# Latent attention, restructured: heads projected in blocks of four, scores unsplit, modulation products on VectorE

## The chip, the cores and the metric

One core of a Trainium2 chip runs the whole network of two layers. The metric is the time of one execution in device microseconds. Before the change it is 1305.78 us, the median of three runs (1305.38 to 1312.1).

## The reference

A diffusion backbone of two layers over 256 context tokens and 256 latent tokens, width 1024, all in fp32. Layer 0 mixes tokens with multi-head latent attention, layer 1 with a Mamba-2 scan; behind each comes a SwiGLU FFN, and a norm ends it. The change touches layer 0's attention and its modulation:

```python
proj = h @ w_in                                   # 512 tokens, 1024 -> 512 + 256 + 32
cq, ckv, kr = split(proj)
q  = (rms_norm(cq, q_norm) @ w_uq)                # 16 heads of 64 + 32 (rotary)
kv = (rms_norm(ckv, kv_norm) @ w_ukv)             # 16 heads: k_nope 64, v 64
# rotary positions on q_rope and kr of the latent tokens only
k = concat(k_nope, broadcast(kr)); q = concat(q_nope, q_rope)
out_x = softmax(q_latent @ k.T / sqrt(96)) @ v @ w_o          # keys: all 512 tokens
out_c = softmax(q_ctx @ k_ctx.T / sqrt(96)) @ v_ctx @ w_o     # keys: 256 context tokens
```

The modulation (shift, scale and gate of each sub-layer) is `silu(c) @ ada_w[i] + ada_b[i]`, 6144 columns for each of two conditioning vectors.

## The kernel before

Everything is kept transposed: features on partitions, 512 tokens on the free axis. A matmul in full precision is made of three fp32r passes (`three`, lines 1498 to 1502): each operand is split into a high and a low part, and low x high, high x high and high x low are summed in a bank. Weights stream through a ring of four buffers: the SP queue loads block n into `raw` (`load`, line 288), ScalarE copies it to `w_hi` (`hi`, line 565), VectorE subtracts to `w_lo` (`lo`, line 963), TensorE uses it and frees it. Each engine's program is an order written out by hand, and engines meet at semaphores.

Attention begins with seven tiles of the input projection (24 matmuls each), two for ckv, one for the rotary key, four for cq. ckv is normed among them. Then the v tiles of all heads are made, while cq's norm runs (a reciprocal of 128x512, a multiplication by the row and a split for each of four tiles), and then the heads follow one after the other. In step i (`head`, lines 771, 1132 and 1714) TensorE projects head i+1 (12 matmuls for q with the swapped rotary features beside it, 6 for k, with 64 columns of weights), transposes the probabilities of head i (12 transposes), does 16 small products for the modulation (`ada_two`, heads 0 to 11), computes the scores of head i+1 in split form (two tiles of 512 keys for the latent queries, two of 256 for the context) and multiplies head i's probabilities with v (`values`, 24 matmuls). ScalarE copies q and k out of the banks, makes their high parts, copies the transposed probabilities, and takes the exponentials of head i+1 with their sums. VectorE rotates q, makes k's low part, splits weights, takes the maxima, inverts the sums and makes the low half of the output. POOL makes q's low part (`q_low`, line 450), scales the probabilities (`scale_probs`, line 437) and copies one head of v.

After the heads follow eight tiles of the output projection, the second norm and the FFN. During the FFN VectorE computes 56 vectors of modulation by `matvec` (line 1039): two products of 128x1024 with a row of silu(c), each with its sum; one such pair gives 128 modulation values for both conditionings. The modulation of layer 0 that attention's output and the FFN's input need is made on TensorE (16 tiles ahead of attention, 24 in the heads).

Of the kernel before, what the change touches and what calls it, by code (L numbers as in the profile page):

```python
# [33 lines left out]
QKD = 96  # L34
# [22 lines left out]
TAB = {"ident": 0, "gt": 128, "lt": 256, "le": 384, "ge": 512, "cos": 640, "sin": 896}  # L57
NTAB = 1152
# [5 lines left out]
HL = HP + 2  # L64
WO = HL + 2 * 15
# [11 lines left out]
ADA1 = 40  # L77
VEC = 56
# [10 lines left out]
def block_cols():  # L89

    cols = [1024] * NBLK
    for i in range(-1, 15):
        n = HP if i < 0 else HL + 2 * i
        cols[n], cols[n + 1] = 512, 128
    cols[DT] = 512
    return cols
# [4 lines left out]

NORM_K = [8, 2, 4, 8, 8, 16, 8, 8]
SPLIT = {3: (5, 6, 7), 4: (7,)}
NB = [sum(k for v, k in enumerate(NORM_K[:w]) if v not in SPLIT) for w in range(len(NORM_K) + 1)]
# [29 lines left out]
def program(nc, a, out):  # L134
# [9 lines left out]
    with ExitStack() as fixed:  # L144
# [20 lines left out]
        gain = [sb(f"gain{i}", [128, 8, 2]) for i in range(4)]  # L165
        bank = [fixed.enter_context(nc.psum_tensor(f"bank{i}", [128, 512], f32)) for i in range(8)]
# [8 lines left out]
        with ExitStack() as ph:  # L175
            Hmh, Hml = (sb(f"mla_h_{p}", [128, KD, TOK], f32r, ph) for p in ("hi", "lo"))
            Oh, Ol = Hmh, Hml
            cq = sb("cq", [128, KQ + KKV, TOK], f32, ph)
            kf = sb("k_rope", [128, TOK], f32, ph)
            cnh, cnl = (sb(f"c_normed_{p}", [128, KQ + KKV, TOK], f32r, ph) for p in ("hi", "lo"))  # L180
            qf = sb("q_f32", [128, TOK], f32, ph)
            qh, ql = (sb(f"q_{p}", [128, TOK], f32r, ph) for p in ("hi", "lo"))
            kh, kl = (sb(f"k_{p}", [128, TOK], f32r, ph) for p in ("hi", "lo"))
            v = sb("v", [128, 4, 64 * HEADS], f32, ph)
            vs = sb("v_head", [128, 2, 4, 64], f32, ph)

            P, rtmp = T[:, 5:8, :], T[:, 4, 0:LAT]
            ada_mla = [cq[:, 2 + 2 * r:4 + 2 * r, :].rearrange("p a n -> p (a n)") for r in range(2)]
# [7 lines left out]
        with ExitStack() as ph:  # L196
            H0h, H0l = (sb(f"ffn0_h_{p}", [128, KD, TOK], f32r, ph) for p in ("hi", "lo"))
            U0h, U0l = (sb(f"ffn0_hidden_{p}", [128, KH, TOK], f32r, ph) for p in ("hi", "lo"))
            vec_w = [T[:, 4 + 2 * r:6 + 2 * r, :].rearrange("p a n -> p (a n)") for r in range(2)]
            crow = sb("silu_c_rows", [128, 2, 1024], f32, ph)  # L200
            vec_prod = sb("matvec_products", [128, 1024], f32, ph)
# [48 lines left out]
        ada_in = [sem(f"ada_in{i}") for i in range(2)]  # L250
# [9 lines left out]
        kr_part, kr_done, kr_hi, kr_lo = sem("kr_part"), sem("kr_done"), sem("kr_hi"), sem("kr_lo")  # L260
        q_cp, rope_part, q_rope, q_hi, q_lo = sem("q_copied"), sem("rope_part"), sem("q_roped"), sem("q_hi_"), sem("q_lo_")
        k_hi, k_lo, v_out, v_mm, v_cp = sem("k_hi_"), sem("k_lo_"), sem("v_out"), sem("v_mm"), sem("v_cp")
# [24 lines left out]
        def _(sp):  # L287
# [9 lines left out]
            def ada(t, r, dst):  # L297

                sp.wait_ge(ada_used, t - 1)
                sp.dma_start(dst[r % 2], one("ada_w", t)).then_inc(ada_in[r % 2], 16)  # L300
# [18 lines left out]
            for t in range(2, 7):  # L319
                load(IN + t, IN + t, 1024, one("w_in", t))  # L320
            for t in range(2):
                load(VB + t, VB + t, 1024, one("w_uv", t))
            load(HP, HP, 512, one("w_uq", 0))
            load(HP + 1, HP + 1, 128, one("w_uk", 0))
            def queries(i, u):
                n, s = HL + 2 * (i - 1), HL + 2 * u
                load(n, s, 512, one("w_uq", i))
                load(n + 1, s + 1, 128, one("w_uk", i))

            def ada_head(i):  # L330
                for r in range(2):
                    ada(ADA0 + 2 * i + r, r, ada_mla)

            queries(1, 0)
            sp.dma_start(crow[:, :, :], a["crow"]).then_inc(crow_in, 16)
            sp.wait_ge(nlo, NB[3])
            with sp.Fori(0, 6) as j:
                for u in range(2):
                    queries(2 * j + u + 2, 1 - u)
                    ada_head(2 * j + u)  # L340
            for u in range(2):
                queries(14 + u, 1 - u)
            for t in range(8):
# [6 lines left out]
            def two(j):  # L350
                for r in range(2):
                    if late(j, 1):
                        sp.wait_ge(vec_used, 2 * j + r - 1)
                    sp.dma_start(vec_w[r], one("vec_w", 2 * j + r)).then_inc(vec_in[r], 16)
# [45 lines left out]
        def _(pool):  # L400
            nc.gpsimd.memset(scm[:, :, :], 0.0).then_inc(ones_set, 1)
            nc.gpsimd.memset(ones[:, :], 1.0).then_inc(ones_set, 1)
            nc.gpsimd.memset(eps[:, :], EPS).then_inc(ones_set, 1)

# [32 lines left out]
            def scale_probs(i, u):  # L437

                pool.wait_ge(rcp, 3 * i + 1)
                if late(i, 2):  # L440
                    pool.wait_ge(o_mm, i - 1)
                nc.gpsimd.tensor_tensor(P[:, 0, :], P[:, 0, :], rs_[:, 0:1].to_broadcast([128, 512]), MUL).then_inc(p_norm, 1)
                nc.gpsimd.tensor_copy(vs[:, u, :, :], v[:, :, ds(64 * i, 64)]).then_inc(v_cp, 1)
# [6 lines left out]
            def q_low(i):  # L450

                pool.wait_ge(q_hi, i + 1)
                nc.gpsimd.tensor_tensor(ql[0:QKD, :], qf[0:QKD, :], qh[0:QKD, :].bitcast(f32), SUB).then_inc(q_lo, 1)  # L453

            pool.wait_ge(v_out, 8)
            q_low(0)
            for i in range(2):
                scale_probs(i, i)
                q_low(i + 1)
            with pool.Fori(1, HEADS // 2 - 1) as i:  # L460
                for u in range(2):
                    scale_probs(2 * i + u, u)
                    q_low(2 * i + u + 1)
            scale_probs(14, 0)
            q_low(15)
            scale_probs(15, 1)
# [94 lines left out]
        def _(act):  # L561
# [136 lines left out]

            whole = [(0, 0, TOK)]
            for t in range(7):  # L700
                act.wait_ge(w_used, IN + t + 1)
                if t == 2:
                    A(kf[64:96, :], bank[0][64:96, :], ACT.Copy).then_inc(proj_out, 1)
                else:
                    c = t if t < 2 else t - 1
                    square(1 if t < 2 else 2, c if t < 2 else c - 2, bank[t % 2][:, :])
                    A(cq[:, c, :], bank[t % 2][:, :], ACT.Copy).then_inc(proj_out, 1)
                hi(IN + t + RING, IN + t + RING)
                if t == 2:
                    act.wait_ge(kr_done, 1)  # L710
                    A(kh[64:96, :], kf[64:96, :], ACT.Copy).then_inc(kr_hi, 1)
                if t == 3:
                    rms(1, TOK, 128 * KKV)
                    his(1, whole, lambda k, c0, c1: cnh[:, k, c0:c1], None)


            for g in range(8):
                if g == 2:
                    rms(2, TOK, 128 * KQ)
# [5 lines left out]
                if g >= 4:  # L725
                    his(2, whole, lambda k, c0, c1: cnh[:, KKV + k, c0:c1], None, [g - 4])
# [3 lines left out]
            def project(i, n, s, between):  # L730

                act.wait_ge(w_used, n + 1)
                if late(i, 1):
                    act.wait_ge(q_lo, i)
                    act.wait_ge(s_mm, 3 * i)
                A(qf[0:QKD, :], bank[0][0:QKD, :], ACT.Copy).then_inc(q_cp, 1)
                act.wait_ge(w_used, n + 2)
                A(kh[0:64, :], bank[1][0:64, :], ACT.Copy).then_inc(k_hi, 1)
                between()
                act.wait_ge(q_rope, i + 1)  # L740
                A(qh[0:QKD, :], qf[0:QKD, :], ACT.Copy).then_inc(q_hi, 1)
                hi(n + 4, s + 4)
                hi(n + 5, s + 5)

            def exps(i, p):

                act.wait_ge(nmax, 3 * i + p + 1)
                if late(i, 1):
# [1327 lines left out]
```

## Time and profile before

| | before |
|---|---|
| median of 3 runs | 1305.78 us |
| profiled execution | 1306.43 us |
| its span | 1304.6 us |
| TensorE busy | 1193.1 us (91%) |
| VectorE busy | 836.5 us (64%) |
| ScalarE busy | 587.9 us (45%) |
| POOL busy | 234.9 us (18%) |
| mean granted TensorE clock | 0.967 |

The profiled execution's own time is 1.8 us more than its span, the time from its first to its last instruction. A busy TensorE is not one at its peak, as ends of matmuls are modelled: where matmuls follow each other, their distance is their cost, not their duration. Attention with its start lies between about 56 and 295 us of the span.

### The profile page before, as it was taken

How to read it: one execution, taken by the hardware profiler on the slowest of the kernel's cores; microseconds unless marked ns; L12 is line 12 of the kernel's file. 1: busy time of each engine (PE TensorE's matmuls, PEld its weight loads, DVE VectorE, ACT ScalarE, POOL GpSimd, SP SyncE). 2: the span in 40 equal slices, each digit the busy share in tenths (PEclk: the TensorE clock that was granted, in tenths of full speed). 3: DMA queues.
4: the chain of work that ended last, by engine and by line, in shares of the span. 5: the costliest groups of instructions: out<-in, count | busy, mean ns of one | idle time of the engine just before them, and what ended most of it. 6: DMA issues, size and time to landing. Idle time of an engine off the chain costs nothing.

```text
span 1304.6 us, 21131 instructions
## 1 busy us (share of the span) xinstructions
PE 1193.1 (91%) x7484; PEld 996.7 (76%) x7484; DVE 836.5 (64%) x1269; ACT 587.9 (45%) x999; POOL 234.9 (18%) x205
## 2 busy tenths in 40 slices
PE   5797999979899999999999879998988778999997
PEld 3575777767888888887888867888844578999996
DVE  0756667653578777775665687877478665655554
ACT  3545666664352222222222466455533254666542
POOL 0102443431200000000111200001278622000011
PEclk9899999999999999999999999999989889999998
DMA  9312333221056555554444123223500025466662
GB/s 377 124 45 95 128 127 127 97 86 65 1 199 220 193 193 193 189 190 156 154 153 141 49 80 106 81 83 124 181 1 1 0 67 192 130 194 193 184 188 79
DMA packets 50472, 169.12 MB, mean 130 GB/s; under 512 B 5488, under 2 KB 8816, under 8 KB 50160
## 3 DMA queue, kind: packets, MB, share of 16 engines
q1 hardware_dynamic: 50416, 168.37, 38.3%
q8 instruction: 36, 0.59, 0.2%
q14 instruction: 20, 0.16, 0.0%
HBM read 167.30 MB, written 1.05 MB: 129 GB/s over the span
## 4 chain that ended last, share of the span: by engine, by line
PE 71%; DVE 9%; issue 9%; POOL 4%; ACT 3%; DMA 2%; SPq 1%; DVEq 0%; POOLq 0%; ACTq 0%
PE bank L1500 22%; PE bank L1502 21%; PE bank L1501 21%; DVE scratch L1419 1%; PE bank L1898 1%; PE bank L1910 1%; DMA raw<-in_w_in 1%; POOL scratch L447 1%; POOL scratch L445 1%; PE bank L1920 1%; DVE w_lo L969 1%; DVE scratch L1304 1%; POOL q_lo L453 1%; ACT w_hi L572 1%; PE bank L1929 1%
## 5 line engine op out<-in xcount | busy, mean ns | idle before, releaser
L969 DVE TENSOR_TENSOR w_lo<-raw,w_hi 128x1024 fp32r<-128x1024 f32 (+1 forms) x242 | 282.3, 1174 | 179.9 <-ACT w_hi L572 179.7
L572 ACT ACTIVATE w_hi<-raw 128x1024 fp32r<-128x1024 f32 (+1 forms) x242 | 234.1, 976 | 267.8 <-PE bank L1502 242.7
L1500 PE MATMUL bank<-ffn_h_lo,w_hi 128*128 128x256 f32 (+1 forms) x736 | 243.9, 331 | 9.1 <-DVE ffn_h_lo L1006 4.9
L1501 PE MATMUL bank<-ffn_h_hi,w_hi 128*128 128x256 f32 (+1 forms) x736 | 243.1, 330 | 0.0
L1502 PE MATMUL bank<-ffn_h_hi,w_lo 128*128 128x256 f32 (+1 forms) x736 | 243.0, 330 | 0.0
L1500 PEld LDWEIGHTS bank<-ffn_h_lo,w_hi 128*128 128x128 f32 x736 | 140.0, 190 | 24.6 <-issue 5.2
L1501 PEld LDWEIGHTS bank<-ffn_h_hi,w_hi 128*128 128x128 f32 x736 | 140.0, 190 | 14.5
L1502 PEld LDWEIGHTS bank<-ffn_h_hi,w_lo 128*128 128x128 f32 x736 | 139.8, 190 | 14.5
L414 POOL TENSOR_TENSOR scratch<-scratch 128x512 f32<-128x512 f32 (+1 forms) x24 | 37.0, 1541 | 599.8 <-ACT scratch L581 599.8
L1500 PE MATMUL bank<-ffn_hidden_lo,w_hi 128*128 128x256 f32 (+1 forms) x374 | 123.0, 329 | 5.8 <-DVE ffn_hidden_lo L1263 5.8
L1500 PE MATMUL bank<-ssd_h_lo,w_hi 128*128 128x256 f32 (+2 forms) x360 | 120.1, 334 | 8.6 <-DVE w_lo L969 5.0
L1502 PE MATMUL bank<-ffn_hidden_hi,w_lo 128*128 128x256 f32 (+1 forms) x374 | 122.5, 327 | 0.0
L1501 PE MATMUL bank<-ffn_hidden_hi,w_hi 128*128 128x256 f32 (+1 forms) x374 | 122.4, 327 | 0.0
L1502 PE MATMUL bank<-ssd_h_hi,w_lo 128*128 128x256 f32 (+2 forms) x360 | 116.9, 325 | 0.0
L1501 PE MATMUL bank<-ssd_h_hi,w_hi 128*128 128x256 f32 (+2 forms) x360 | 116.8, 325 | 0.0
L1304 DVE SCALAR_TENSOR_TENSOR scratch<-conv_in,par,scratch 128x512 f32<-128x512 f32 (+1 forms) x96 | 67.9, 707 | 29.0 <-ACT scratch L845 22.4
L1500 PEld LDWEIGHTS bank<-ssd_h_lo,w_hi 128*128 128x128 f32 (+1 forms) x360 | 68.7, 191 | 16.7 <-DVE w_lo L969 5.4
L1500 PEld LDWEIGHTS bank<-ffn_hidden_lo,w_hi 128*128 128x128 f32 x374 | 70.6, 189 | 13.5 <-DVE ffn_hidden_lo L1263 6.4
L1501 PEld LDWEIGHTS bank<-ffn_hidden_hi,w_hi 128*128 128x128 f32 x374 | 70.8, 189 | 7.1
L1502 PEld LDWEIGHTS bank<-ffn_hidden_hi,w_lo 128*128 128x128 f32 x374 | 70.6, 189 | 7.1
L1046 DVE SCALAR_TENSOR_TENSOR matvec_products<-scratch,silu_c_rows 128x1024 f32<-128x1024 f32 x56 | 73.8, 1317 | 0.0
L1502 PEld LDWEIGHTS bank<-ssd_h_hi,w_lo 128*128 128x128 f32 (+1 forms) x360 | 68.5, 190 | 6.6
(245 smaller groups left out, 2222.1 us busy)
## 6 DMA issues: line engine op xcount, KB each, us to landing
raw<-in_w SPq DMA_DIRECT2D x120, 512.0 KB, 4.4
scratch<-in_vec_w SPq DMA_DIRECT2D x56, 512.0 KB, 3.4
cq<-in_ada_w SPq DMA_DIRECT2D x24, 512.0 KB, 4.4
raw<-in_w_xbc SPq DMA_DIRECT2D x24, 512.0 KB, 3.4
ada_start<-in_ada_w SPq DMA_DIRECT2D x8, 1024.0 KB, 17.4
raw<-in_w_z SPq DMA_DIRECT2D x16, 512.0 KB, 3.6
raw<-in_w_so SPq DMA_DIRECT2D x16, 512.0 KB, 4.3
raw<-in_w SPq DMA_DIRECT2D x16, 384.0 KB, 4.0
```

What stands on the lines that cost most here:

```text
L414: nc.gpsimd.tensor_tensor(T[:, ACC[w], 0:n], before, T[:, (b + k) % 2, 0:n], ADD).then_inc(sq_used, 2 if k == 1 else 1)
L445: nc.gpsimd.tensor_tensor(P[:, 1, :], P[:, 1, :], rs_[:, 1:2].to_broadcast([128, 512]), MUL).then_inc(p_norm, 1)
L447: nc.gpsimd.tensor_tensor(P[:, 2, :].rearrange("p (a k) -> p a k", a=2), P[:, 2, :].rearrange("p (a k) -> p a k", a=2), rs_[:, 2:4].unsque ...
L453: nc.gpsimd.tensor_tensor(ql[0:QKD, :], qf[0:QKD, :], qh[0:QKD, :].bitcast(f32), SUB).then_inc(q_lo, 1)
L572: A(wh[s % RING][:, 0:c], raw[s % RING][:, 0:c], ACT.Copy).then_inc(w_hi, 1)
L969: V.tensor_tensor(wl[s % RING][:, 0:c], raw[s % RING][:, 0:c], wh[s % RING][:, 0:c].bitcast(f32), SUB).then_inc(w_lo, 1)
L1046: V.scalar_tensor_tensor(prod, vec_w[r], 1.0, crow[:, s, :], MUL, MUL, accum_out=m).then_inc(done, 1)
L1304: V.scalar_tensor_tensor(acc, up[:, u, seg, r:r + 256], par[:, ds(PAR["conv_w"] + 5 * t + r, 1)], acc, MUL, ADD).then_inc(conv_tap, 1)
L1419: last = V.scalar_tensor_tensor(T[:, 2 + h // 4, q], cbf[:, 4 * c + g, :], dt[:, 2 + c, GH * g + h:GH * g + h + 1], T[:, 4 + h // 4, q], M ...
L1500: mm(o, lh, rl, start=first, stop=False)
L1501: mm(o, lh, rh, start=False, stop=False)
L1502: return mm(o, ll, rh, start=False, stop=final)
```

## The change

- **Blocks of four heads.** Sixteen blocks of 512 weight columns replace the 32 uneven ones. A group of four heads has a block A and a block B (the 64 plain q features of two heads each), C (the rotary q features of all four) and K (k of the four, in two halves). Blocks 0 to 4 are projected ahead of the heads; step i projects block i+5 into bank 7, up to step 10. q has six slots, k four.
- **Rotation** of four heads at once: TensorE swaps the halves with a permutation matrix (`swap`), VectorE multiplies and adds (`rotate`).
- **Unsplit scores**: q and k stay in fp32, a score tile is one fp32 matmul. The high and low parts of q and k, and POOL's part in them, go.
- **No norm of cq by rows**: `q_norm`'s gain is applied in the copy out of the bank, the tokens' inverse root becomes the scale of the exponential and of the negated maximum (`q_scale`, `q_neg`). Its sum is 8 fp32 matmuls of one column.
- **Modulation on VectorE**: the 24 tiles of products on TensorE become 24 vectors of `matvec`: eight in the input projection and behind it, twelve in the heads (each step but 1, 5, 9 and 15), four between the output tiles. SiLU of the rows of c moves from the end of attention to its start.
- **Order in a step**: TensorE computes the scores of head i+1 first, then transposes head i, projects, multiplies values. ScalarE takes copies of the transposed probabilities and exponentials in turn. The loops over heads are written out.

```diff
 # TensorE
+            def head(i):
+                b = i + 5
+                kind, g = HEAD_BLOCKS[b] if b < 16 else (None, None)
+                if i < 15:
+                    for p in range(3):
+                        scores(i + 1, p)
                 for p in range(3):
                     transpose_probs(i, p)
+                if kind:
+                    bank7_free(b)
+                if kind == "K":
+                    k_tile(b, 0, bank[7])
+                elif kind:
+                    q_tile(b, bank[7])
+                values(i)
+                if kind == "K":
+                    pe.wait_ge(k_out, 4 * g + 2)
+                    k_tile(b, 1, bank[7])
+                elif kind == "C":
+                    swap(b, bank[7])
 ...
-                    last = three(bank[p][:, :], qh[0:QKD, q], ql[0:QKD, q], kh[0:QKD, :], kl[0:QKD, :], True, True)
+                    last = mm(bank[p][:, :], qf[0:QKD, q, qs], kf[0:QKD, i % 4, :], start=True, stop=True)
 ...
             for t in range(1, 7):
                 if t >= 2:
                     pe.wait_ge(proj_out, t - 1)
+                if t >= 5:
+                    pe.wait_ge(cq_lo, t - 4)
 # ScalarE
+            def head(i):
+                for p in range(3):
+                    pt_split(i, p)
+                    if i < 15:
+                        exps(i + 1, p)
+                if i + 5 < 16:
+                    project_out(i + 5, (bank[7], bank[7]))
                 act.wait_ge(o_mm, i + 1)
 ...
+            def project_out(b, banks):      # ends, for every block, with
+                if b + 4 < 16 + 4:
+                    hi(HP + b + 4, HP + b + 4)
 # VectorE
+            def head(i, v):
+                if i < 15:
                     maxes(i + 1, 0)
                     maxes(i + 1, 1)
                     inverse(i + 1, 0)
                     maxes(i + 1, 2)
                     inverse(i + 1, 1)
                     inverse(i + 1, 2)
+                if i + 5 < 16 + 4:
+                    if i + 5 < 16:
+                        lo(HP + i + 5 + 4, HP + i + 5 + 4)
+                    if i in ROPE_STEPS:
+                        rotate(HEAD_BLOCKS[i + 5][1], bank[7])
+                if v is not None:
+                    matvec_mla(v)
                 for r in range(2):
                     dve.wait_ge(o_hi, 2 * i + r + 1)
 ...
+            def rotate(g, b):
+                V.tensor_tensor(rope_c[:, :], qr[:, CTX:TOK], tabv("cos", LAT), MUL).then_inc(rope_part, 1)
+                dve.wait_ge(q_perm, g + 1)
+                V.tensor_tensor(rope_s[:, :], b[:, 0:LAT], tabv("sin", LAT), MUL).then_inc(rope_part, 1)
+                for u in range(4):
+                    V.tensor_tensor(qf[64:96, q_slot(h + u), CTX:TOK], rope_c[r, :], rope_s[r, :], ADD).then_inc(q_rope, 1)
 ...
 # VectorE, input projection, for t in range(7), behind lo(IN + t + RING)
+                if t >= 3:
+                    V.scalar_tensor_tensor(cnl[:, KKV + k, :], bank[t % 2][:, :], par[...], cnh[:, KKV + k, :].bitcast(f32), MUL, SUB).then_inc(cq_lo, 1)
                 if t == 3:
                     norm(1, ...)
+                if t < 6:
+                    matvec_mla(t)
 # SP queue, in the heads
+            for i in range(HEADS):
+                b = i + 8
+                if b < 16:
+                    load(HP + b, HP + b, 512, one("w_heads", b))
+                elif i - 8 < 4:
+                    load(WO + i - 8, WO + i - 8, 1024, one("w_o", i - 8))
+                if i in VEC_STEPS:
+                    vec(at, vec_mla[:, at % 2, :])       # waits for the matvec two before
```

## Rows read from the trace of the kernel before

**Rows 1.** The page's chain of waits: shares of the span by engine.

```profile
PE 71%; DVE 9%; issue 9%; POOL 4%; ACT 3%; DMA 2%; SPq 1%; DVEq 0%; POOLq 0%; ACTq 0%
```

**Rows 2.** Stretch over heads 1 to 12: length, busy PE, PEld, DVE, ACT, POOL, clock, DMA.

```profile
133.44:269.00 135.56, 125.08 (x1119) 99.20 (x1119) 91.79 (x217) 85.68 (x215) 56.27 (x60) 1.00 0.34 120
```

**Rows 3.** Timeline of one head, TensorE: start us, duration us, engine, line, operation, count.

```profile
152.84 1.03 PE L1692 MATMUL bank<-tab,scratch 128*128 128x128 f32 x8
...
154.24 1.08 PE L1533 MATMUL bank<-cq,silu_c_and_mod_rows 128*32 128x128 f32 x32
156.03 0.50 PE L1500 MATMUL bank<-k_lo,q_hi 96*128 96x512 f32 x1 [0.70 <-POOL q_lo L453]
...
158.44 0.66 PE L1708 MATMUL bank<-probs_t,v_head 128*64 128x128 f32 x8
159.90 0.50 PE L1500 MATMUL bank<-c_normed_lo,w_hi 128*128 128x512 f32 x1
...
164.19 1.03 PE L1692 MATMUL bank<-tab,scratch 128*128 128x128 f32 x8
```

**Rows 4.** The same head on VectorE, ScalarE and POOL.

```profile
157.03 0.69 DVE L1118 TENSOR_REDUCE softmax_max<-bank 128x1 f32<-128x512 f32 x1
158.08 0.69 ACT L753 ACTIVATE scratch<-bank,softmax_negmax 128x512 f32<-128x512 f32 x1 [1.77 <-DVE softmax_negmax L1122]
158.90 0.69 ACT L753 ACTIVATE scratch<-bank,softmax_negmax 128x512 f32<-128x512 f32 x1
159.30 1.04 POOL L442 TENSOR_TENSOR scratch<-scratch,softmax_inv 128x512 f32<-128x512 f32 x1 [3.32 <-DVE softmax_inv L1130]
160.40 0.47 ACT L757 ACTIVATE scratch<-bank,softmax_negmax 128x256 f32<-128x256 f32 x1 [0.72 <-DVE softmax_negmax L1122]
161.44 0.78 ACT L785 ACTIVATE mla_h_hi<-bank 64x256 f32 x2
```

**Rows 5.** Chain of waits in order: one fp32 matmul of 512 columns, as two passes.

```profile
64.31 0.86 PE bank L1633 x2
```

**Rows 6.** Timeline of ScalarE in the input projection.

```profile
79.99 0.59 ACT L707 ACTIVATE cq<-bank 128x512 f32<-128x512 f32 x1
80.47 1.06 ACT L572 ACTIVATE w_hi<-raw 128x1024 fp32r<-128x1024 f32 x1
...
82.98 0.63 ACT L572 ACTIVATE w_hi<-raw 128x512 fp32r<-128x512 f32 x1
```

**Rows 7.** Timeline of VectorE in the first FFN.

```profile
377.42 1.22 DVE L1046 SCALAR_TENSOR_TENSOR matvec_products<-scratch,silu_c_rows 128x1024 f32<-128x1024 f32 x1
...
379.71 1.22 DVE L969 TENSOR_TENSOR w_lo<-raw,w_hi 128x1024 fp32r<-128x1024 f32 x1
380.85 0.69 DVE L1260 TENSOR_TENSOR scratch<-bank,scratch 128x512 f32<-128x512 f32 x1
```

**Rows 8.** VectorE's last work of attention.

```profile
293.68 0.88 DVE L1150 TENSOR_TENSOR mla_h_lo<-bank,mla_h_hi 64x256 fp32r<-64x256 f32 x2 [4.57 <-ACT mla_h_hi L785]
```

**Rows 9.** A rotary operation of the head of rows 3.

```profile
153.26 0.42 DVE L1107 TENSOR_TENSOR q_f<-q_f,scratch 32x256 f32<-32x256 f32 x1
```

**Rows 10.** VectorE with two SBUF inputs, in the scan, while POOL works.

```profile
985.00 2.06 DVE L1428 TENSOR_TENSOR W<-decay,scratch 128x1024 f32<-128x1024 f32 x1
```

**Rows 11.** Start of attention: kv norm on VectorE, first v tile, a table load.

```profile
74.15 3.35 DVE L974 RECIPROCAL scratch<-scratch 128x512 f32<-128x512 f32 x1
...
78.98 1.35 DVE L1004 TENSOR_TENSOR c_normed_lo<-scratch,c_normed_hi 128x512 fp32r<-128x512 f32 x2
...
87.41 0.40 PE L1500 MATMUL bank<-w_lo,c_normed_hi 128*128 128x512 f32 x1
...
110.47 1.28 ACT L753 ACT_TABLE_LOAD   x1
```

**Rows 12.** TensorE after the q norm, and the stretch behind its wait.

```profile
102.47 0.50 PE L1500 MATMUL bank<-c_normed_lo,w_hi 128*128 128x512 f32 x1 [2.15 <-DVE c_normed_lo L1004]
...
104.00:108.00 4.00, 4.00 (x13) 2.83 (x13) 0.26 (x1) 0.59 (x1) 0.00 (x0) 0.67 0.91 289
```

More of the change, by code:

```diff
@@ L76 @@
 ADA0 = 16
-ADA1 = 40
-VEC = 56
+VEC = 80
+VEC_HEADS = 8
+VEC_OUT = 20
+VEC_FFN = 24
 RING = 4
@@ L91, in block_cols @@
     cols = [1024] * NBLK
-    for i in range(-1, 15):
-        n = HP if i < 0 else HL + 2 * i
-        cols[n], cols[n + 1] = 512, 128
+    for n in range(HP, HP + 16):
+        cols[n] = 512
     cols[DT] = 512
@@ L448, in scale_probs @@
                                         rs_[:, 2:4].unsqueeze(2).to_broadcast([128, 2, 256]), MUL).then_inc(p_norm, 1)
[L450 to L466, printed above, removed]
+            for i in range(HEADS):
+                scale_probs(i)
             accumulate(3, TOK)
@@ new lines, in _ @@
+                    pe.wait_ge(root, DONE[2])
+                    pe.wait_ge(sq_used, b + KQ - 1 - USED[2])
+                    pe.wait_ge(sq_ready, b + KQ)
+                    for t in range(4):
+                        tt = slice(128 * t, 128 * t + 128)
+                        mm(bank[6][:, t:t + 1], T[:, ACC[2], tt], ones[:, 0:1], start=True, stop=False)
+                        last = mm(bank[6][:, t:t + 1], T[:, (b + KQ - 1) % 2, tt], ones[:, 0:1], start=False, stop=True)
+                    last.then_inc(sum_done, 1)
@@ L1727, in head @@
-                if u and ada:
-                    turn_ready(4 + j)
-                if more:
-                    scores(i + 1, 2)
-                if u and ada:
-                    turn()
-                values(i, u)
-            project(0, HP, HP)
-            pe.wait_ge(kr_lo, 1)
+                if kind:
[5 more added lines that the diff above has]
+                values(i)
@@ L1737, in _ @@
+            q_tile(4, bank[7])
+            swap(3, bank[2])
+            pe.wait_ge(kr_cp, 3)
+            pe.wait_ge(k_out, 4)
+            pe.wait_ge(q_nope, 4)
             for p in range(3):
                 scores(0, p)
-            head(0, 0, 0)
-            head(1, 0, 1)
-            with pe.Fori(1, 6) as j:
-                head(2 * j, j, 0)
-                head(2 * j + 1, j, 1)
-            head(12, 6, 0)
-            head(13, 6, 1)
-            head(14, 7, 0)
-            head(15, 7, 1)
+            for i in range(HEADS):
+                head(i)
```

426 lines of the change are left out of this document (222 added, 204 removed).

## The prediction

> **What bounds the kernel now.** I read the chain of waits first, for whose work ends last: TensorE carries 71% of it and VectorE 9% [rows 1]. Then the table of stretches over heads 1 to 12 of attention, the stage that the change rewrites: in 135.56 us TensorE is busy 125.08, 92%, VectorE 68%, ScalarE 63% [rows 2]. So a head costs what TensorE has to do in it, and the timeline of one head says what that is [rows 3]. Transposes to transposes it lasts 164.19 - 152.84 = 11.35 us: 12 transposes (1.4), the AdaLN products with their gap (1.5), 0.7 of waiting for POOL's low part of q, scores (2.1 and a table turn), values 1.46 (158.44 to 159.90), the 18 matmuls of the next projection 4.29 (0.24 each, 2.8 for twelve). The third view is what the other engines do in the same head [rows 4], for there the step of the changed kernel has to be put together: its TensorE work falls so far that another ring must be looked for.
>
> **What the change takes from TensorE and gives it.** AdaLN products: -1.08 of matmuls in each of 12 heads [rows 3]. Projection: 18 matmuls per head become 48 per four heads, 2.8 us per head instead of 4.2: -1.4. Scores unsplit: three fp32r passes of 0.24 become one fp32 matmul, which in this trace is recorded as two passes and holds TensorE for 0.86 us at 512 columns [rows 5]; a head needs two of 512 and two of 256: 2.6 instead of 2.1, so +0.5. One swap of 256 columns per four heads: +0.1. TensorE's own work of a step with a projection is then 2.6 + 1.5 + 2.8 + 1.5 = 8.4 us, without one 5.6. If TensorE stayed the bound, some 2.9 us would be gained in each of 11 steps. I don't think it does.
>
> **The ring that takes its place.** In a step of the changed kernel VectorE's order is: maxima of head i+1, inverses, `lo` of the weight block, matvec, low half of the output, and then the maxima of head i+2. ScalarE's order is: copies of the transposed probabilities and exponentials in turn, the two to five copies out of bank 7 (`project_out`), and `hi` of the same weight block, for which VectorE's `lo` waits. So nothing of head i+2 starts before `lo`, matvec and output low are through. Worked out from x, the start of the first maximum:
> - to the first exponential 158.08 - 157.03 = 1.05; two exponentials of 0.82 each to the next instruction (158.90 - 158.08); the last, in two halves, 161.44 - 160.40 = 1.04 [rows 4]; between them two copies of 512 columns at 80.47 - 79.99 = 0.48 [rows 6], say 0.50: x + 4.75.
> - two copies out of bank 7, 1.0; `hi` of 512 columns 0.63 [rows 6]; `lo` of 512 columns, half of 380.85 - 379.71 = 1.14; matvec 379.71 - 377.42 = 2.29 [rows 7]; output low 0.88 [rows 8]: x + 10.1, with waits between engines 10.2.
> TensorE's 8.4 us fit beside it: values at x + 3.9, the next scores to x + 8, transposes to x + 9.5, projection to x + 12.3, and then 2 us of waiting until the next values.
> So a step with blocks A or B is 10.2 us (steps 0, 3, 4, 7, 8: 51.0). A step with block C has one copy and four small ones instead of two (+0.9), and instead of the matvec a rotation of six operations of 0.42 [rows 9], some 2.5: 11.3 (steps 1, 5, 9: 33.9). A step with block K projects its second half only after ScalarE has copied the first out of the one bank: 6 matmuls (1.4) and two more copies, with the hand-overs 2.9: 13.1 (steps 2, 6, 10: 39.3). From step 7 on the block loaded is one of the output projection with 1024 columns: `hi` 1.06 instead of 0.63, `lo` 1.14 instead of 0.6, +1.0 in four steps: 4.0. Steps 11 to 13 have only a matvec: 4.75 + 0.3 + 2.29 + 0.88 = 8.2, and there the matvec meets POOL's third scaling (1.04, [rows 4]). What that costs the trace does not show for this pair; the nearest row is a two-input VectorE operation of 1024 columns beside POOL, 2.06 against 1.22 alone [rows 10]; bounds 0 and 0.85 a step, I take 0.6: 26.4 for the three. Step 14 and the last head, with values waiting for the output low of head 14 and two engines after them: 11.9. Sum 166.5 us, and 1.5 for slower clock in the K steps (below): 168.
>
> **The start of the stage.** In the tiles of the input projection VectorE now does a matvec after each, and of a q tile it also makes the low part out of the bank (0.7). TensorE's last tile waits for the second of these. The kv norm there can begin its reciprocal at about 75.0 instead of 74.15: either the 0.7 in front of it, or the square-root table that SiLU of c displaced, 1.28 [rows 11]. It takes 80.33 - 74.15 = 6.2 us, to 81.2; matvec to 83.5; `lo` to 84.65; the low part to 85.35. In the kernel before the last tile starts at 87.41 - 5.6 = 81.8 [rows 11]. TensorE stands 3.6 us, and runs perhaps 2 us of the next at the lower clock: +4.6, so the v tiles start at 92.0 instead of 87.4. Then 12.2 us of v tiles (12.9 before with a norm sum twice as wide), 5 blocks of 2.8, the swap, one rotated head: first scores at 119.9; but VectorE rotates three more heads and splits two blocks first, so the first maximum is at 122.4. Head 0's softmax is three rounds in a row, 6.0; head 1's first exponential waits for the scores of head 1 and the first transposes behind them: as if x were 129.5. What goes here is the q norm: 3.35 of reciprocal and the row of values and low parts behind it, for which TensorE waited 2.15 at 102.47 [rows 12]; late in its place are the five blocks.
> Attention ends at 129.5 + 168 = 297.5 us instead of 293.68 + 0.88 = 294.6 [rows 8]: **+2.9 us**.
>
> **What is free.** POOL loses the copy of v and q's low part, neither on the new ring. Four matvecs between the output tiles: add 0.9, `lo` 1.14, matvec 2.29 is 4.3 of 5.6 us per tile; cover gone, they would cost the excess only. On SP's queue each vector load waits for the matvec two before it and the weight load behind it waits too; block i+9 is issued by the end of step i-2, a step and more before ScalarE wants it, so it costs nothing as long as a load lands within 10 us. The FFN does the same 56 matvecs as before. SiLU of c sits in ScalarE's wait for the first tile pair. Against the profiled execution (1306.43 us, span 1304.6) the sum is 1309.3; that execution stood 0.65 above the median shown, so I predict **1308.6 us**.
>
> **Where rows and the skill are weighed.** At 102.47 TensorE had stood for 2.15 us, and in the stretch that follows its granted clock was 0.67, between its levels of 2.4 and 1.2 GHz [rows 12]; waits of 0.7 per head left it at 1.00 [rows 2, 3]. The changed step has a wait of 2 to 3 us, so I expect the lower clock in part of the steps; as TensorE has 2 us of slack there, only the K steps pay (0 to 1.4 each, I take 0.5).
> The Trainium skill (TensorE: Matmul & The Clock Gate, section HAM oscillation) says that a loop whose every round waits falls back to the low clock every time. By it each step would pay; that is the second rival, whose price is made from rows.
> The Trainium skill (GPSIMD Engine Reference, its table of specifications) says GpSimd shares its SBUF interface with VectorE operations that have two SBUF inputs. The trace agrees with 2.06 against 1.22 us.
>
> **Rivals.**
> - TensorE stays the bound, because its waits overlap better than my ring lets them. Eleven steps of 8.4, 1.4 to 2 more in the K steps, 7 for the short ones: attention ends some 29 us earlier, 1277 us. For it: the shares of rows 2, and 4 us of work gone. Against: the order of VectorE's instructions, which closes the ring.
> - The clock, on the other side (slower than before). If TensorE works whole steps at 1.2 GHz, a plain step is not 8.4 but 8.4 + 8.4/2 or more, 12 to 13 us, and passes the ring of 10.2; it decides from the point at which more than about 4 us of work per step are at the low level. At 2 us more in each of 14 steps: +28, 1334 us.
> - My ring holds, but the start or the steps are off by up to 1 us each: it is 1297 to 1321, so it spills over both bounds of what can be told.
> - The change does in the start what it should but block K is hidden: -9, 1300.
>
> **How the numbers follow.** Ring as summed with its own range 1299 to 1318: 0.66; small errors that make it faster than 1299 (K hidden, contention nil): 0.12; TensorE bound: 0.10; clock: 0.12. A measurement of this kernel tells from no change what is over 0.5%, 6.5 us. Of the first case 0.43 lie within it and 0.23 above; so faster 0.22, within 0.43, slower 0.35. Range: the unknown costs reach from -10 (contention, K clock and start's clock at nothing, K hidden in part) to +10; out to the rivals until two in ten are left: 1292 to 1324.
>
> **What would show it.** Right: steps of 10 to 11 us with 13 at heads 3, 7 and 11 by the spacing of the values matmuls; VectorE waiting for `w_hi` once a step and busy from there to the next maximum; ScalarE's first exponential waiting for VectorE's negated maximum, not for TensorE; TensorE idle 2 us before each values group; a wait of 3 to 4 us before the last input tile. Wrong: TensorE above 90% busy over attention; a step under 9 us; a granted clock under 0.8 over the whole of it; or waits of VectorE for a vector load.

## The result, and the profile after

The changed kernel takes **1331.96 us** (1331.81 to 1333.36, four runs) against 1306.21 us for the kernel before (four runs): ratio 1.019, interval 1.0159 to 1.022. The forecast was 1308.6 with a range of 1292 to 1324. It is 23 us too low, and the time lies above the range. The profiled execution took 1331.81 us, span 1330.0.

The first view is the page's chain of waits after, shares by engine, which answers [rows 1]:

```profile
PE 68%; DVE 15%; ACT 8%; issue 5%; DMA 1%; SPq 1%; POOL 1%; DVEq 0%; ACTq 0%; POOLq 0%
```

VectorE and ScalarE have taken from TensorE and POOL, as forecast. The second view is the table of stretches of the kernel after, from the first maximum of head 1 to that of head 13, twelve steps (start and end, length, busy PE, PEld, DVE, ACT, POOL, granted clock, DMA share, GB/s). It answers [rows 2]:

```profile
131.98:275.03 143.05, 112.40 (x665) 83.89 (x666) 85.99 (x198) 86.66 (x204) 39.38 (x37) 0.89 0.15 52
```

A head went from 11.35 us to 143.05 / 12 = 11.9, and TensorE from 92% busy at clock 1.00 to 79% at 0.89. The third view is the timeline of a plain step after (start us, duration us, engine, line, operation; the idle time before it and what ended that):

```profile
169.97 0.69 DVE L1153 TENSOR_REDUCE softmax_max<-bank 128x1 f32<-128x512 f32 x1
...
170.89 0.78 ACT L776 ACTIVATE scratch<-bank,softmax_negmax,q_scale 128x512 f32<-128x512 f32 x1 [2.86 <-DVE softmax_negmax L1157]
...
174.45 1.21 ACT L765 ACTIVATE q_heads<-bank 64x512 f32<-64x512 f32 x2
...
175.57 0.62 ACT L571 ACTIVATE w_hi<-raw 128x512 fp32r<-128x512 f32 x1
176.22 0.69 DVE L983 TENSOR_TENSOR w_lo<-raw,w_hi 128x512 fp32r<-128x512 f32 x1 [1.43 <-ACT w_hi L571]
...
176.82 1.22 DVE L1060 SCALAR_TENSOR_TENSOR vec_products<-vec_weights,silu_c_rows 128x1024 f32<-128x1024 f32 x1
...
179.23 0.88 DVE L1184 TENSOR_TENSOR mla_h_lo<-bank,mla_h_hi 64x256 fp32r<-64x256 f32 x2
...
180.13 0.69 DVE L1153 TENSOR_REDUCE softmax_max<-bank 128x1 f32<-128x512 f32 x1
```

That is the ring of the forecast, link by link, in 180.13 - 169.97 = 10.16 us where 10.2 was summed. So the miss is not in the ring's plain step. Spacings of these first maxima give all steps (us, forecast in brackets): the first plain one, counted as the forecast counts it (from 1.05 before the first exponential of head 1, at 134.33), 10.2 and the other two 10.2 and 10.1 (10.2), with 1024-wide weights 11.1 and 11.0 (11.2); C 11.6, 11.6, 12.6 (11.3, 11.3, 12.3); K 13.8, 14.8, 14.8 (13.6, 13.6, 14.6). Then comes what was not forecast: short steps 8.9, **12.2**, 9.7 (8.8 each), and 14.3 to the first output tile (11.9). Together 176.8 instead of 168. The start adds 4.9: the first exponential of head 1 at 135.38 instead of 130.5.

TensorE's timeline in the short steps shows why:

```profile
269.73 1.12 PE L1751 MATMUL bank<-probs_t,v 128*64 128x128 f32 x8 [6.23 <-ACT probs_t L792]
270.64 1.92 PE L1754 MATMUL bank<-probs_t,v 128*64 128x128 f32 x16
272.49 3.78 PE L1721 MATMUL bank<-k_heads,q_heads 96*128 96x512 f32 x4
276.06 1.91 PE L1725 MATMUL bank<-k_heads,q_heads 96*128 96x256 f32 x4
277.77 1.65 PE L1735 MATMUL bank<-tab,scratch 128*128 128x128 f32 x8
```

After 6.23 us of waiting the scores of head 13 take 3.78 us; after a wait of 1.08 us (head 10, at 232.74) they take 1.98. The transposes behind head 13's scores come late, and ScalarE's copies and exponentials wait for those.

Attention explains 13.7 us of the miss. Nearly all the rest is in code that the diff doesn't touch: the first addition of the output projection comes at 317.1 instead of 302.0, 15.1 us later, and the kernel ends 25.4 later. Stage by stage, the second layer's 256-column matmuls grow: its gated FFN goes from 191.8 to 200.4 us, its z tiles from 47.2 to 50.1. (The output projection adds 1.0 and the output of the scan 1.5; the first norm and FFN take 2.8 off.) Two stretches, TensorE alone, of the kernel before (a stretch of the first FFN with 512-column matmuls, and one of the last FFN with 256 columns):

```profile
440.00:500.00 60.00, 60.00 (x259) 1.00 0.55 190
1140.00:1200.00 60.00, 60.00 (x532) 1.00 0.62 192
```

and of the kernel after:

```profile
440.00:500.00 60.00, 60.00 (x258) 1.00 0.58 195
1140.00:1200.00 60.00, 60.00 (x509) 1.00 0.62 198
```

With 512 columns it does what it did (258 matmuls, 259 before). With 256 the engine is busy throughout, at full clock, with about as much DMA traffic, and does 4% less.

### The profile page after: what moved, and what is told of

It is laid out like the page before. It is cut to its first block, busy times and chain, and to the rows that moved or that the text cites. A ratio compares the mean times of both kernels' runs of the same rounds, so it can differ in the third digit from the quotient of the medians.

```text
span 1330.0 us, 19400 instructions
## 1 busy us (share of the span) xinstructions
PE 1194.1 (90%) x6954; PEld 993.3 (75%) x6954; DVE 857.8 (64%) x1295; ACT 589.2 (44%) x986; POOL 214.7 (16%) x174
## 3 DMA queue, kind: packets, MB, share of 16 engines
HBM read 166.31 MB, written 1.05 MB: 126 GB/s over the span
## 4 chain that ended last, share of the span: by engine, by line
PE 68%; DVE 15%; ACT 8%; issue 5%; DMA 1%; SPq 1%; POOL 1%; DVEq 0%; ACTq 0%; POOLq 0%
PE bank L1535 20%; PE bank L1536 19%; PE bank L1537 19%; DVE scratch L1339 5%; DVE scratch L1454 1%; PE bank L1968 1%; PE bank L1956 1%; ACT scratch L776 1%; ACT scratch L859 1%; DMA raw<-in_w_in 1%; ACT w_hi L571 1%; DVE w_lo L983 1%; PE bank L1978 1%; PE bank L1754 1%; PE bank L1721 1%
## 5 line engine op out<-in xcount | busy, mean ns | idle before, releaser
L983 DVE TENSOR_TENSOR w_lo<-raw,w_hi 128x1024 fp32r<-128x1024 f32 (+1 forms) x226 | 270.2, 1198 | 210.8 <-ACT w_hi L571 210.7
L571 ACT ACTIVATE w_hi<-raw 128x1024 fp32r<-128x1024 f32 (+1 forms) x226 | 230.8, 1023 | 273.2 <-PE bank L1537 252.4
```

Source lines behind the costliest of these rows:

```text
L571: A(wh[s % RING][:, 0:c], raw[s % RING][:, 0:c], ACT.Copy).then_inc(w_hi, 1)
L983: V.tensor_tensor(wl[s % RING][:, 0:c], raw[s % RING][:, 0:c], wh[s % RING][:, 0:c].bitcast(f32), SUB).then_inc(w_lo, 1)
```

## Experiments

Theories: **place**: the new tile `eps_q` [128, 1] takes 32 bytes ahead of every phase's buffers (the other fixed tiles that grew or were added take multiples of 512), and that slows the 256-column matmuls. **Ring**: VectorE and ScalarE set the steps, with the matvec's 2.3 us in them. **Clock**: half clock after TensorE's waits costs the short steps and part of the K steps and the start. Each has its rival in the expectations.

**1. The kernel before with 32 bytes more.**

```diff
         gain = [sb(f"gain{i}", [128, 8, 2]) for i in range(4)]
+        pad = sb("pad", [128, 1])
```

> The kernel before, with one tile of one column (4 bytes a partition) that nothing uses, placed where the changed kernel places eps_q: all buffers of the phases behind it move by 32 bytes. After the change the groups of 256-column matmuls in the second layer, which the diff does not touch, ran at 87 for every 10 us instead of 90 to 91, and the layer lost about 10 us. Theory placement (the move of 32 bytes makes the 256-column fp32r matmuls slower): 1306 + 10 = 1316 us, 87 matmuls per 10 us in the second layer's gated FFN, nothing lost in attention. Rival (the slower matmuls come from what the attention of the changed kernel leaves behind, in the clock or elsewhere): 1306 us, 90 to 91 per 10 us.

Measured: 1317.54 us, ratio 1.0086 (1.0048 to 1.0124). 509 matmuls per 60 us in the last FFN, as after, and attention as before (first output tile added at 301.8 us, 302.0 before). A tile that nothing reads costs about 10 us (0.5 to 1.2% by the interval).

**2. The same with 64 bytes**, `[128, 16]`.

> The kernel before, with an unused tile of 16 columns in the same place: the buffers of the phases move by 64 bytes. Theory placement, in the form that a start on a multiple of 64 bytes is what counts: 1306 us, as before. Rival form (the start within 128 bytes counts, and before it happens to be the good one or the bad one): 1300 or less, or 1310 or more.

Measured: 1305.52 us, 0.9982 (0.9963 to 1.0). Neither form holds as put: the time is the first form's only because two changes cancel. The first FFN is faster (266 instead of 259 per 60 us) and the last slower (502). Each width has its own best place.

**3. The changed kernel with `eps_q` of 128 bytes**, `[128, 32]`.

> The changed kernel with eps_q 32 columns wide (128 bytes), of which it uses the first: the phases' buffers stand again where they stood, within 128 bytes. Theory placement: 1332 - 10 = 1322 us, the second layer at 90 to 91 matmuls per 10 us, the delay of its end against its start gone (+15 to 16 us at the output projection, +15 to 16 at the end). Rival (something left behind by the attention): 1332 us.

Measured: 1321.4 us, 1.0118 (1.008 to 1.0156). The time came as the theory had it, the reason did not: the last FFN stays at 512 per 60 us, the first goes to 264. A place 128 bytes on is a third one, not the old one. Of the 14.3 us between the two profiled executions 3.3 lie ahead of the output projection, where the order is the same: TensorE's clock fell in other places (step 12 took 9.5 us instead of 12.2). No run separates that from the move of the buffers. This is the base of the next run and of run 5.

**4. The matvec early**, its two products in VectorE's waits for exponentials.

```diff
                     maxes(i + 1, 2)
+                    if v is not None:
+                        matvec_half(v, 0)
                     inverse(i + 1, 1)
+                    if v is not None:
+                        matvec_half(v, 1)
                     inverse(i + 1, 2)
...
-                if v is not None:
-                    matvec_mla(v)
```

> The changed kernel with eps_q as in the run before, and the matvec of a head cut into its two products, the first put behind the third maximum of the next head, the second behind its second inverse, where VectorE waits for exponentials. Theory ring (VectorE from the weights' low half through matvec and output low to the next maxima sets the plain step, 10.2 us): the matvec's 2.3 us leave the ring in 12 steps, which then come to 8.0 to 8.6 us, TensorE's own work, the K steps to 11.5: 12 x 1.8 = 22 us less than the run before, 1300 us. Rival (TensorE with its clock sets them, VectorE is only late because its inputs are): steps stay at 10, 1318 to 1322 us. Rival (POOL's scalings and the matvec meet now and stretch each other, 2.05 instead of 1.14 and 1.96 instead of 1.04 us): half the gain, 1311 us.

Measured: 1306.65 us, 0.9988 (0.9972 to 1.0003): 15 us less than run 3. VectorE's timeline of a plain step:

```profile
174.80 0.69 DVE L1163 TENSOR_REDUCE softmax_max<-bank 128x1 f32<-128x512 f32 x1
...
177.89 1.21 DVE L1070 SCALAR_TENSOR_TENSOR vec_products<-vec_weights,silu_c_rows 128x1024 f32<-128x1024 f32 x1
...
182.60 0.69 DVE L1163 TENSOR_REDUCE softmax_max<-bank 128x1 f32<-128x512 f32 x1
```

7.8 us instead of 10.1: the matvec was on the ring with its whole price, 2.3. The gain is under the 22 us expected. The K steps gave 2.1 to 3.4 us each and the wide ones 1.7, but the short ones nothing (29.6 us for the three instead of 28.1; the scores of head 13 took 3.78 us), and the three C steps, which have no matvec, took 0.9 more together. POOL's scaling beside the matvec stretches:

```profile
171.33 1.94 POOL L459 TENSOR_TENSOR scratch<-scratch,softmax_inv 128x512 f32<-128x512 f32 x1 [1.31 <-DVE softmax_inv L1175]
```

against 1.04 alone [rows 4]; the matvec beside it stays at 1.2.

**5. Matmuls that nothing reads in TensorE's waits**, on run 3. They write a bank that is free there; the results of the kernel don't depend on them.

```diff
-                pe.wait_ge(pt_out, 3 * i + 3)
                 if i:
                     pe.wait_ge(o_lo, 2 * i)
+                filler(FILL[i], bank[3])
+                pe.wait_ge(pt_out, 3 * i + 3)
...
+            FILL = [0, 1, 7, 4, 1, 3, 7, 4, 2, 4, 7, 10, 4, 4, 4, 1]
...
+                for _ in range(n):
+                    mm(o[:, 0:256], tabv("ident"), tabv("cos", LAT), start=True, stop=True)
...
                 if kind == "K":
+                    filler(2, bank[2])
```

> The changed kernel with the wide eps_q (1321.4 us), and with fp32 matmuls of 256 columns on the identity, whose results nothing reads, put where TensorE waits in a head: 1 to 4 of them before the values matmuls of plain steps, 7 in K steps with 2 more before the second half of K, 10 in the step behind the last K, 4 in the short steps. Theory clock (TensorE's waits of 2 to 6 us bring the half clock, under which scores and transposes of the short steps, the K steps' matmuls and values take twice as long): granted clock over 125 to 300 us from 0.88 to 0.97 or more, the scores of heads 13 to 15 at 1.98 instead of 3.78 us, steps 12 and last each 2 to 3 us shorter, K steps 0.5: 1313 to 1316 us. Rival (the clock is low where the ring of VectorE and ScalarE covers it, and the fillers only delay): 1321 to 1325 us.

Measured: 1317.22 us, 1.0056 (1.0036 to 1.0075), between what the two theories expected and nearer to the clock's. Attention ends 5.6 us earlier than in run 3 by the traces. TensorE over 125 to 300 us, first run 3:

```profile
125.00:300.00 175.00, 133.24 (x783) 0.88 0.17 56
```

then with the fillers:

```profile
125.00:300.00 175.00, 154.03 (x964) 0.98 0.17 58
```

and the short step of above in run 3, without fillers:

```profile
271.51 1.12 PE L1751 MATMUL bank<-probs_t,v 128*64 128x128 f32 x8 [6.12 <-ACT probs_t L792]
272.42 1.92 PE L1754 MATMUL bank<-probs_t,v 128*64 128x128 f32 x16
274.27 2.40 PE L1721 MATMUL bank<-k_heads,q_heads 96*128 96x512 f32 x4
```

and with them (ten fillers, of which the first line shows the second half):

```profile
265.64 2.32 PE L1763 MATMUL bank<-tab 128*128 128x256 f32 x10
267.89 0.66 PE L1752 MATMUL bank<-probs_t,v 128*64 128x128 f32 x8
268.38 1.04 PE L1755 MATMUL bank<-probs_t,v 128*64 128x128 f32 x16
269.35 1.98 PE L1721 MATMUL bank<-k_heads,q_heads 96*128 96x512 f32 x4
271.18 1.03 PE L1725 MATMUL bank<-k_heads,q_heads 96*128 96x256 f32 x4
```

Values at 0.66 and 1.04 us instead of 1.12 and 1.92, scores at 1.98 instead of 2.40 (3.78 in the changed kernel's own trace); those of the next two heads took 3.06 and 1.98 in run 3 and take 1.98 now. More work on TensorE, less time: the clock theory holds. It also shows that the price is not fixed: behind a wait of about 6 us the same scores took 3.78 us in one execution and 2.40 in another.

**6. `eps_q` of 512 bytes**, `[128, 128]`, on run 4.

> The kernel with the matvec early (1306.65 us), and eps_q 128 columns wide, so that the buffers behind it move by a multiple of 512 bytes against the kernel before instead of by 128. So far: back-to-back matmuls of 512 columns came at 259 per 60 us with the buffers where they were before or 32 bytes on, 264 at 128 bytes and 266 at 64; those of 256 columns at 532, 509, 511 and 502. Theory place (the rate depends on where the buffers start within some hundred bytes, each place with its own pair of rates): 259 and 532 again; the first FFN 6 us longer, the second layer 9 us shorter, 1303 to 1304 us. Rival (it differs from run to run, or only the 32 bytes count): 264 and 511, 1306.7 us.

Measured: 1304.27 us, 0.9968 (0.9938 to 0.9998). The time alone doesn't tell this from run 4, but the rates do. By the two stretches it is the old place:

```profile
440.00:500.00 60.00, 60.00 (x259) 1.00 0.53 181
1140.00:1200.00 60.00, 60.00 (x532) 1.00 0.62 189
```

The rates followed the start of the buffers within 512 bytes, whatever the kernel (matmuls per 60 us, 512 and 256 columns):

| moved by, within 512 bytes | kernels | 512 col. | 256 col. |
|---|---|---|---|
| 0 | before; runs 6, 12 | 259, 259, 259 | 532, 532, 532 |
| 32 | changed; run 1 | 258, 259 | 509, 509 |
| 64 | run 2 | 266 | 502 |
| 64 for the first layer, 0 for the second | run 9, below | 266 | 532 |
| 128 | runs 3, 4 | 264, 263 | 512, 511 |

**7. The ring of C and K steps**, on run 4. VectorE rotates before it splits weights; the second half of K goes to bank 2 without waiting for the copies of the first; ScalarE makes the output's high half before it copies that half; the split of the weights loaded in a K step moves into the next step.

```diff
-                    if i + 5 < 16:
-                        lo(HP + i + 5 + 4, HP + i + 5 + 4)
                     if i in ROPE_STEPS:
                         rotate(HEAD_BLOCKS[i + 5][1], bank[7])
...
+                    if i + 5 < 16 and i not in K_STEPS:
+                        lo(HP + i + 5 + 4, HP + i + 5 + 4)
...
-                    pe.wait_ge(k_out, 4 * g + 2)
-                    k_tile(b, 1, bank[7])
+                    k_tile(b, 1, bank[2])
```

> The kernel with the matvec early (1306.65 us), and the ring of the C and K steps mended: in C steps VectorE rotates before it makes the weights' low half; in K steps the second half of K goes to bank 2 without a wait for the copies of the first, ScalarE makes the output's high half before it copies that half, and VectorE makes the weights' low half a step later. Theory ring: C steps 1.5 us shorter each, K steps 1.5 to 2.5: 3 x 1.5 + 3 x 2 = 10 us, 1296 to 1299 us. Rival (TensorE's own work of 8.4 us and its half clock after waits set these steps by now): under 4 us, 1303 to 1306 us.

Measured: 1294.46 us, 0.9893 (0.9868 to 0.9917): 12 us less than run 4, a little more than the theory's 10.

**8. The start**, on run 4. The matvec of the fourth input tile moves behind the low half of the next query tile.

```diff
-                if t < 6:
+                if t < 6 and t != 3:
+                    if t == 4:
+                        matvec_mla(3)
                     matvec_mla(t)
```

> The kernel with the matvec early (1306.65 us), and the matvec of the fourth input tile put behind the low half of the next query tile, for which TensorE's last input tile waits. Theory (that wait, 3.6 to 4 us, is part of the loss): the wait falls to 1.3 to 1.7 us and the tile runs at the full clock, v tiles 3 us earlier, 1303 to 1304 us. Rival (the start is set by what VectorE has to do up to the first maxima): 1306.7 us.

Measured: 1298.84 us, 0.992 (0.9903 to 0.9938), 7.8 less where the theory expected 3. TensorE's last input tile in the changed kernel, in run 4 (in brackets the time that the engine stood before it):

```profile
86.25 0.77 PE L1535 MATMUL bank<-mla_h_lo,w_hi 128*128 128x512 f32 x1 [5.50 <-issue]
...
86.76 0.77 PE L1547 MATMUL bank<-mla_h_lo,w_hi 128*128 128x512 f32 x1 [5.71 <-issue]
```

and in this one:

```profile
83.89 0.47 PE L1549 MATMUL bank<-mla_h_lo,w_hi 128*128 128x512 f32 x1 [2.70 <-ACT c_normed_hi L711]
```

The first maximum comes at 120.29 us instead of 126.31: 6.0 us for a matvec of 2.3. The stretches with TensorE alone say where the other half is. In run 4:

```profile
75.00:85.00 10.00, 6.05 (x27) 1.00 0.02 5
85.00:95.00 10.00, 8.24 (x24) 0.66 0.53 188
```

and in this run:

```profile
75.00:85.00 10.00, 7.30 (x33) 1.00 0.00 0
85.00:95.00 10.00, 10.00 (x54) 1.00 0.61 199
```

The last input tile starts 2.9 us earlier (83.89 instead of 86.76) and takes 5.6 us instead of 8.5, because with the shorter wait the clock stayed at 1.00: the half clock behind the wait had cost as much as the part of the wait that went.

**9. The kernel before with 64 bytes ahead of the first layer's buffers alone**, `sb("pad0", [128, 16], f32, ph)` in its FFN phase and the same as `padm` in attention.

> The kernel before, with an unused tile of 16 columns (64 bytes) ahead of the buffers of attention and of the first FFN alone; the second layer's stay where they are. Theory place: each stage keeps the rate that its own place had in the runs so far, so 266 matmuls of 512 columns per 60 us in the first FFN (259 before) and still 532 of 256 columns in the second layer: 9 us less than before, 0.993 of it. Rival (rates belong to the whole program and not to a stage's buffers, or the gain of one stage is lost in another as with all buffers moved): 0.998 to 1.000.

Measured: 1299.35 us, 0.9925 (0.9891 to 0.9959). Its stretches:

```profile
440.00:500.00 60.00, 60.00 (x266) 1.00 0.58 199
1140.00:1200.00 60.00, 60.00 (x532) 1.00 0.63 195
```

Each stage keeps the rate of its own place, as the theory had it, and the best place tried for either width stands in one kernel.

**10. Runs 4, 7, 8, the 512 bytes and the 64 bytes together.**

> What the runs so far found, together: matvec early, mended C and K steps, the matvec of the fourth input tile moved, eps_q 128 columns wide and the 64 bytes ahead of the first layer's buffers. Summed from the single runs against 1306.65 of the kernel with the matvec early: ring -12.2, start -7.8, second layer's place -2.4, first layer's place -8 to -9: 1276 us. Rival (ring and start share their gain, as TensorE's 8.4 us per step bound what is left): 1283 us.

Measured: 1274.37 us, 0.9736 (0.9701 to 0.9771). The single gains add up to within 2 us, in an interval of 4.5 us either way, and the rival's 1283 us lies outside it.

**11. The same with fillers** in the waits that are left.

> The run before with matmuls that nothing reads in TensorE's remaining waits: 3, 2 and 1 of them ahead of the scores of head 1, 4 before the values of the K and the short steps. Theory clock: heads 0 to 1 and the short steps lose their half clock, 3 to 4 us less than the run before, 1272 us. Rival (by now no wait is long enough for the clock to matter): the same to 1 us.

Measured: **1269.5 us**, 0.9703 (0.9669 to 0.9737), 4.9 us less than run 10, with 3 to 4 expected; the two intervals overlap, so the time alone doesn't show the gain. The granted clock does: over 150 to 275 us it is 1.00 in every stretch of 25, where run 10 has 0.73 to 1.00. This version beats the kernel before by 3.0% and the changed one by more.

**12. The changed kernel's own order with only place and clock taken out**: `eps_q` [128, 128] and the fillers of run 5, with 3, 2 and 1 ahead of head 1's scores.

> The changed kernel in its own order (matvec late, start as it is), with only the two causes taken out that the prediction had left out or priced too low: eps_q 128 columns wide, so that the second layer's buffers stand where they stood, and the matmuls that nothing reads in TensorE's waits, with 3, 2 and 1 more ahead of the scores of head 1. Theory (the forecast's sum of steps was right but for these two and some 3 us of the start): 1317.2 - 2.4 - 1.5 against a kernel before at 1310.4 in the same runs, ratio 1.001 to 1.004. Rival (something else of the order of 5 us or more is still missing): ratio over 1.006.

Measured: 1312.85 us, 1.004 (1.0019 to 1.0062). The estimate is the upper end of what the theory allowed, and the interval reaches just past the rival's 1.006. It is 3.9 us above the kernel before, where the prediction had 2.8. The agreement is closer than it should be: the 2.8 held 1.5 us for the clock in the K steps, which the fillers take away too, and in the traces attention still ends 8.5 us later than before (303.16 instead of 294.61), where 2.9 was forecast.

## Why the prediction was wrong

Slower by over 0.5%, to which it gave 0.35, is what happened. The sums of the ring were right; the price of the clock was too low, the start was late, and a term was missing.

- **Ring in place of TensorE**: right. Plain, C and 1024-wide steps came within 0.4 us each, and run 4 shows the matvec on it with its full 2.3 us. The rival in which TensorE stays the bound is dead, the one in which K is hidden too.
- **"As TensorE has 2 us of slack there, only the K steps pay"**: this is the step that failed in attention. The price was weighed for the projecting steps alone. In the short steps a whole head's scores (1.98 us at full clock, 3.78 at half), transposes and values stand between two waits, and transposes are on the ring there. Terms mis-sized: short steps and last head 6.7 us more than summed, K steps 1.6 beyond the 1.5 set aside for their clock, C steps 1.0, plain steps 0.5 less: 8.8. The size is that of one execution: in run 3's trace, with the same order, the steps are 5.1 over the sum, and the short ones with the last head 1.6 of it. Fillers (run 12) end attention 8.0 us earlier than here. The Trainium skill (TensorE: Matmul & The Clock Gate, section HAM oscillation) describes a loop in which every round does short work and then waits long for its data, and starts every round at the low clock. The trace agrees in part for heads 12 to 15: waits of 2.16 to 6.23 us come in every round, and the scores of heads 13 and 15 take 3.78 us, those of head 14 2.67. It does not for the projecting steps: from 225 to 250 us they wait 1.08 and 2.58 us, and the granted clock is 1.00.
- **The start**: forecast +4.6 us for stall and clock up to the v tiles, at 92.0; they began at 94.20. TensorE's last input tile began at 86.25 instead of 85.35, after a stand of 5.5 us and not 3.6 (the tile before it had ended at 80.8, a microsecond sooner than summed), and took 7.95 us, the first half of it at half clock, where the forecast allowed 5.6 + 1. The first maximum came at 125.29 instead of 122.4. Head 0's three rounds took 6.7 instead of 6.0; that is not the clock, for run 12 with fillers there has 6.7 too. From head 1's first maximum to its first exponential it took 3.4 instead of 2.1, and that is the clock: 2.0 in run 12. In all 4.9 us. Run 8 brings the first maximum forward by 6.0 with one matvec moved, more than the miss, since the forecast had counted most of the stall.
- **"What is free"**: the sum took it for granted that unchanged code keeps its time. It doesn't: 32 bytes cost about 10 us in the second layer. No row of the kernel before could have shown it, since a trace holds one place only; it was a missing term and no rival named it. Runs 1, 6, 9 and 12 show it. The contention price of 0.6 a step in the short steps was near but low: the second product took 2.05 us instead of 1.22 in all four steps in which it met POOL, 0.83 each, close to the upper bound of 0.85.
- **The clock rival** (1334 us) came within 2 us of the time by another way than its own: it had every step pay 2 us, and the plain ones paid nothing.

In us: 13.7 in attention (start 4.9, steps 8.8), as the trace has them, leave 9.7 for what is behind it of the 23.4 between 2.8 forecast and 26.2 measured against the three runs shown. Run 12, without the place and with fillers, is at 3.9. What stays of the miss there is in attention: by its trace 5.7 us over the forecast's 297.5, of which 3.7 stand in the first maximum (126.08 instead of 122.4), 0.7 in head 0's rounds and the rest in the steps; behind attention it takes 12.0 us less than the changed kernel and 3.2 less than the kernel before, 1.4 of these in the first output tile, whose matmuls the kernel before began at half clock (0.63 us recorded, 0.40 after); the other 1.8 are not explained. That run 12's 3.9 lies so near the 2.8 is luck in part. So place and clock carry most of the miss, and a late start the rest.

What stays open: why a place within 512 bytes sets the rate. The weights' buffers did not move in any of these kernels, so it is the moving side's place, or the distance between the two; no run tells these apart, nor whether a width other than 256 or 512 has other best places.

## What to carry to other kernels

When work leaves the bounding engine, write the new ring out as an order of instructions, as here, and then ask of every wait that it leaves on TensorE what stands behind it at half clock: the price is the next matmuls twice as long wherever they feed the ring, and fillers or one moved operation give it back. Work that has no deadline, like the matvec, goes into the waits inside the ring (between two dependent operations) and not at its end. Before a change is judged, look whether untouched stages kept their matmul rate per stretch; if not, a small tile may have moved their buffers, and a pad per phase is a knob of its own, worth 0.75% (0.4 to 1.1) in the kernel before.

## What the runs showed of the hardware that was not expected

- With TensorE always busy at granted clock 1.00, fp32r matmuls came at 0.2256 to 0.2317 us (512 columns) and 0.1128 to 0.1195 us (256 columns), by the place of the stages' buffers within 512 bytes, which hold the moving operand; of the four places tried the one that is best for 512 columns is worst for 256 (64 bytes: 266 and 502 per 60 us).
- Fp32 filler matmuls of 256 columns, 1.89 us for four, shortened attention by 5.6 us where TensorE waited. They aren't free where they outlast the wait: the last head took 12.3 us with them and 11.8 without.
- A matvec product (VectorE, two inputs in SBUF) and POOL's scaling don't share the time: whichever starts second takes longer by about what the first has left. In the changed kernel POOL starts 0.16 us behind the first product and takes 1.96 us instead of 1.04; the second product starts while POOL works and takes 2.05 instead of 1.22. It is so in all four steps in which they meet:

```profile
283.16 1.22 DVE L1060 SCALAR_TENSOR_TENSOR vec_products<-vec_weights,silu_c_rows 128x1024 f32<-128x1024 f32 x1
283.32 1.96 POOL L461 TENSOR_TENSOR scratch<-scratch,softmax_inv 128x512 f32<-128x512 f32 x1 [0.54 <-DVE softmax_inv L1165]
...
284.31 2.05 DVE L1060 SCALAR_TENSOR_TENSOR vec_weights<-vec_weights,silu_c_rows 128x1024 f32<-128x1024 f32 x1
```

  In run 4 POOL starts 0.15 us behind the second product in each of twelve steps, so POOL alone pays (1.94 us) and the product stays at 1.2.
